# Four of twelve modulation blocks ahead of the first norm, the other eight in the merges, and each block on two column groups

## What is computed

```
mod = silu(c) @ w_mod[l] + b_mod[l]            # c: (1, 1024), w_mod[l]: (1024, 6144)
mod_c = silu(c_ctx) @ w_mod[l] + b_mod[l]
sh1, sc1, g1, sh2, sc2, g2 = split(mod, 6)
h = rmsnorm(x, norm1[l]) * (1 + sc1) + sh1     # first norm
q, k, v of three attention branches, gates = split(h @ w_in[l])
x = x + g1 * (sum over branches of sigmoid(gate_n) * (o_n @ w_branch[l][n])) @ w_out[l]
h2 = rmsnorm(x, norm2[l]) * (1 + sc2) + sh2    # second norm
x = x + g2 * moe(h2)                           # 16 experts, two for each token
```

## Time and profile before

| | |
|---|---|
| median of 3 runs | 1875.71 us (1874.19 to 1879.04) |
| the profiled execution | 1875.32 us, span 1873.7 us |
| mean granted TensorE clock | 0.964 |
| PE busy | 1696.4 us, 91% |
| DVE, ACT, POOL busy | 463.4, 339.6, 132.2 us |
| DMA | 396.74 MB, mean 212 GB/s |
| w_mod: loads | 24 of 2048 KB |
| w_mod: matmul passes (L1369) | 384, busy 170.6 us |

### The profile page before, as it was taken

How to read it: one execution, slowest core, us unless ns; L and a number is a source line. 1 busy time by engine, 2 the same in 40 slices (tenths; PEclk the granted TensorE clock), 3 DMA queues, 4 the chain that set the end, 5 groups by cost and what they waited for, 6 DMA issues and landing times. The chain is left out here.

```text
span 1873.7 us, 15998 instructions
## 1 busy us (share of the span) xinstructions
PE 1696.4 (91%) x6163; PEld 758.0 (40%) x6163; DVE 463.4 (25%) x1206; ACT 339.6 (18%) x759; POOL 132.2 (7%) x219
## 2 busy tenths in 40 slices
PE   7999998889999999999999989998799949987871
PEld 1244445554444445244444324445544424432220
DVE  0324016760011123210110145207601140011003
ACT  1011117770000012010010012017600111010001
POOL 0110000010000000210000020000200010001001
PEclk9999999999999998999999999999999969998886
DMA  9971323012213044899999997243234177999992
GB/s 337 369 250 51 90 96 141 14 28 68 78 57 134 0 147 146 332 372 357 391 387 393 395 382 232 91 113 146 55 117 155 45 279 271 323 370 385 380 393 99
DMA packets 178194, 396.74 MB, mean 212 GB/s; under 512 B 23694, under 2 KB 27822, under 8 KB 177928
## 3 DMA queue, kind: packets, MB, share of 16 engines
q1 hardware_dynamic: 160256, 327.17, 49.0%
q0 software_dynamic: 17136, 66.13, 9.5%
q10 hardware_dynamic: 724, 2.38, 0.3%
HBM read 373.27 MB, written 34.18 MB: 217 GB/s over the span
## 5 line engine op out<-in xcount | busy, mean ns | idle before, releaser
L1418 PE MATMUL bank<-ring_sb,HT_sb 128*128 128x512 f32 x672 | 297.0, 597 | 2.7 <-ACT HT_sb L701 1.5
L1483 PE MATMUL bank<-ring_sb,HT_sb 128*128 128x512 f32 x576 | 253.3, 592 | 1.4 <-ACT QR_sb L792 1.4
L1598 PE MATMUL bank<-ring_sb,QR_sb 128*64 128x512 f32 x608 | 149.7, 649 | 42.0 <-DMA ring_sb<-w_e_up 42.0
L1418 PEld LDWEIGHTS bank<-ring_sb,HT_sb 128*128 128x128 f32 x672 | 126.2, 192 | 150.2 <-issue 148.3
L1369 PE MATMUL bank<-ring_sb,cT_sb 128*2 128x512 f32 x384 | 170.6, 605 | 1.6 <-DMA ring_sb<-w_mod 1.6
L1483 PEld LDWEIGHTS bank<-ring_sb,HT_sb 128*128 128x128 f32 x576 | 109.3, 190 | 138.7 <-issue 136.8
L1487 PE MATMUL bank<-ring_sb,QR_sb 128*128 128x512 f32 x288 | 129.5, 592 | 0.0
L1598 PEld LDWEIGHTS bank<-ring_sb,QR_sb 128*64 128x64 f32 x608 | 49.8, 149 | 128.0 <-issue 127.9
L1459 PE MATMUL bank<-WK_sb,KR_sb 128*64 128x128 f32 x960 | 68.3, 280 | 36.3 <-ACT WK_sb L802 35.5
L1584 PE MATMUL bank<-ring_sb,QR_sb 128*128 128x512 f32 x208 | 94.2, 606 | 3.4 <-ACT QR_sb L838 3.4
L1614 PE MATMUL bank<-ring_sb,QR_sb 128*128 128x512 f32 x208 | 91.8, 594 | 0.0
(11 more groups left out here) (209 smaller groups left out, 1333.1 us busy)
## 6 DMA issues: line engine op xcount, KB each, us to landing
ring_sb<-w_e_gate SPq DMA_DIRECT2D x32, 2048.0 KB, 18.7
ring_sb<-w_e_up SPq DMA_DIRECT2D x32, 2048.0 KB, 21.0
ring_sb<-w_e_down SPq DMA_DIRECT2D x32, 2048.0 KB, 20.4
ring_sb<-w_mod SPq DMA_DIRECT2D x24, 2048.0 KB, 12.5
ring_sb<-w_in SPq DMA_DIRECT2D x22, 2048.0 KB, 15.7
MB_sb<-mod_d POOLq DMA_DIRECT2D x16, 512.0 KB, 8.2
ring_sb<-w_branch SPq DMA_DIRECT2D x8, 1024.0 KB, 10.1
ring_sb<-w_out SPq DMA_DIRECT2D x4, 2048.0 KB, 10.3
```

Source lines behind the costliest of these rows:

```text
L1418: ins = mm(bank[j % 4][:, :], HT[:, k, P * t:P * t + P], WR[slot][:, k], start=(k == 0), stop=(k == KD - 1))
L1483: ins = mm(bank[i % 2][:, :], HT[:, k, P * t:P * t + P], WR[wg][:, k], start=(k == 0), stop=(k == KD - 1))
L1598: ins = mm(bank[0][HALF * side:HALF * side + HALF, :], hgT[q % 2][:, k, 0:HALF], WR[slot][:, k], start=(k == 0), stop=(k == KD - 1))
```

## The change

Four things are done together.

- **c.** c and c_ctx are loaded with eight neighbouring elements in each partition, straight into the form that cT needs; the eight transposing matmuls go. A partition's rows of w_mod are then eight neighbouring ones ("(p k) n" in place of "(k p) n"). ScalarE issues all loads of X ahead of Silu. The waits of SP on c, tab and `AHEAD` go.
- **Two column groups.** A block's matmuls 0 to 3 write partitions 0 and 1 of the bank, and 4 to 7 partitions 64 and 65, in turn. VectorE adds both halves, one addition more per row. This holds for all 24 blocks.
- **The first four blocks alone.** Blocks 0 to 3 come first. Their rows are spread to 128 partitions by matmuls with a column of the identity as weights, repeated 128 times (`spread_row`, two for each row, into banks 4 to 7), and copied by ScalarE into `modb`; neither a store nor a load. The first norm of layer 0 follows, and its transposes fall between the first jobs of the projection, as in layer 1.
- **The other eight in the merges.** Block 4 + i // 2 runs after merge job i, for i = 1, 3, ... 15 (jobs count from 0), on PE, VectorE and in the order of loads. POOL loads their bias and gain after attention, stores the eight rows, and then loads gout and modb. The rows of blocks 0 to 7 of layer 1 get a place each. POOL waits for the stores of layer 1's rows ahead of `load_modb(1, 0)`.

The diff, cut:

```diff
-AHEAD = 3
-H1_ROWS = (6, 7, 8, 9)
+FIRST = 4
-MOD_BANK = (0, 1, 2, 3, 0, 1, 2, 3, 0, 1, 2, 3, 0, 4, 5, 0, 4, 5, 3, 4, 0, 1, 2, 3)
+MOD_BANK = (0, 1, 2, 3, 4, 5, 4, 5, 4, 5, 4, 5, 0, 4, 5, 0, 4, 5, 3, 4, 0, 1, 2, 3)
+def mods_after(l, i):
+    return [FIRST + i // 2] if l == 0 and i % 2 and i // 2 < NMOD - FIRST else []
...
     for l in range(L):
         order = []
-        names = [("mod", l, j) for j in range(MOD_GAP * l, NMOD)]
+        names = [("mod", l, j) for j in (range(MOD_GAP, NMOD) if l else range(FIRST))]
         names += [(u, l) for u, _ in proj_units(l)]
-        names += [(x, l) for n in range(NB) for x in (f"wb{n}", f"g{n}0", f"g{n}1")] + [("wo0", l), ("wo1", l)]
+        i = 0
+        for n in range(NB):
+            names.append((f"wb{n}", l))
+            for half in range(2):
+                names.append((f"g{n}{half}", l))
+                for t in queries(l):
+                    names += [("mod", l, j) for j in mods_after(l, i)]
+                    i += 1
+        names += [("wo0", l), ("wo1", l)]
...
-        mrow = [KR[0:2, c0:c0 + CW] for c0 in (3 * D, 3 * D + CW, D, D + CW)]
-        crow = X[0:2, 3, :]
+        mrow0 = mrow + [KR[0:2, 5 * D + CW * (j % 2):5 * D + CW * (j % 2) + CW] for j in range(FIRST, NMOD)]
+        mrow1 = [HT[0:2, j, :] for j in range(MOD_GAP)] + [mrow[j % 2] for j in range(MOD_GAP, NMOD)]
...
-                    if l == 0 and i == 1:
-                        eng.wait_ge(c_in, 32)
-                        eng.wait_ge(tab_in, 16)
-                    if l == 0 and AHEAD <= i < NMOD:
-                        eng.wait_ge(mod_mm, i - AHEAD + 1)
...
                 eng.wait_ge(pv_mm, M0 + M)
+                if l == 0:
+                    load_bmod(0, MB[0:2, 0:4 * D], FIRST)
+                    load_norm(0, 1)
+                    for j in range(FIRST, NMOD):
+                        store_mod(0, j)
                 mod_stored(NMOD * (l + 1))
                 load_gout(l, 2)
                 load_modb(l, 3)
...
+                    mod_stored(NMOD + MOD_GAP)
                     load_modb(1, 0)
...
-            eng.wait_ge(cT_mm, 1)
-            act(cT[:, :, :].rearrange("p k s -> p (k s)"), bank[7][:, 0:2 * KD], ACT.Silu).then_inc(cT_ready, 1)
...
+                if l == 0:
+                    for i in range(2 * FIRST):
+                        j, strm = divmod(i, 2)
+                        part, half = divmod(j, 2)
+                        eng.wait_ge(row_mm, i + 1)
+                        act(modb[:, strm, 1 - part, CW * half:CW * half + CW], bank[4 + i % 4][:, :], ACT.Copy)\
+                            .then_inc(row_copied, 1)
...
-                eng.wait_ge(mod_mm, i + 1)
-                n = 2 if l else 4
-                if i >= n:
-                    eng.wait_ge(mod_store[(i - n) % 4], 16 * ((i - n) // 4 + 1))
+                eng.wait_ge(mod_mm, 2 * (i + 1))
+                if j >= (MOD_GAP if l else FIRST) + 2:
+                    last_use = stored(l, j - 2)
+                    eng.wait_ge(mod_store[last_use % 4], 16 * (last_use // 4 + 1))
+                made = [bank[MOD_BANK[i]][HALF * side:HALF * side + 2, :] for side in range(2)]
+                link(tt(row, made[1], b, ALU.add))
                 if part in (1, 4):
-                    link(tt(row, made, b, ALU.add))
+                    link(tt(row, row, made[0], ALU.add))
                     stt(row, row, 1.0, nrow[l][part // 4][:, CW * half:CW * half + CW], ALU.add, ALU.mult)\
                         .then_inc(mod_row, 1)
...
+            for t in range(NT):
+                eng.wait_ge(row_copied, 2 * FIRST - 1 + t // NLAT)
+                modulated(t, hn[t % 2])
...
-                for k in range(KD):
-                    ins = mm(bank[use][0:2, :], cT[:, k, :], WR[slot][:, k], start=(k == 0), stop=(k == KD - 1))
-                ins.then_inc(mod_mm, 1)
+                for k in range(KD // 2):
+                    for side in range(2):
+                        ins = mm(bank[use][HALF * side:HALF * side + 2, :], cT[:, KD // 2 * side + k, :],
+                                 WR[slot][:, KD // 2 * side + k], start=(k == 0), stop=(k == KD // 2 - 1))
+                        if k == KD // 2 - 1:
+                            ins.then_inc(mod_mm, 1)
+            def spread_row(j):
+                eng.wait_ge(mod_row, j + 1)
+                for strm in range(2):
+                    i = 2 * j + strm
+                    if i >= 4:
+                        eng.wait_ge(row_copied, i - 3)
+                    mm(bank[4 + i % 4][:, :], ident[0:2, strm:strm + 1].broadcast_to([2, P]), mrow0[j],
+                       start=True, stop=True).then_inc(row_mm, 1)
+            for j in range(FIRST):
+                modulation(j)
+                if j == 0:
+                    eng.wait_ge(tab_in, 16)
+                else:
+                    spread_row(j - 1)
+            spread_row(FIRST - 1)
+            eng.wait_ge(row_copied, 2 * FIRST)
...
                     ins.then_inc(branch_mm, 1)
+                    for j in mods_after(l, i - before(merge_jobs, l)):
+                        modulation(NMOD * l + j)
```

More of the change, by code:

```diff
@@ L296, in build @@
         gq_in = sem("gq_in")
-        cT_mm = sem("cT_mm")
+        row_mm = sem("row_mm")
+        row_copied = sem("row_copied")
         cT_ready = sem("cT_ready")
@@ L517, in store_mod @@
                 eng.wait_ge(mod_row, i + 1)
-                dma(mod_d[l, :, CW * j:CW * j + CW], mrow[i % (2 if l else 4)]).then_inc(mod_store[i % 4], 16)
+                dma(mod_d[l, :, CW * j:CW * j + CW], mrow1[j] if l else mrow0[j]).then_inc(mod_store[stored(l, j) % 4], 16)
             def mod_stored(count):
                 for i in range(4):
-                    eng.wait_ge(mod_store[i], 4 * count)
+                    eng.wait_ge(mod_store[i], 4 * (count - FIRST))
             def load_modb(l, first):
@@ L529, in load_modb @@
                             .then_inc(modb_in, 16)
-            load_bmod(0, QR[0:2, 0:6 * D], 0)
+            load_bmod(0, QR[0:2, 0:2 * D], 0)
             load_norm(0, 0)
[L533 to L539, removed]
             dma(masks[:, :], t_in["masks"]).then_inc(const_in, 16)
@@ L716, in _ @@
                         copy_h(NT * 2 * l + t - 1, t - 1)
+                if l == 0:
[5 more added lines that the diff above has]
+                            .then_inc(row_copied, 1)
                 for t in range(NT - 1 if l else 0, NT):
                     copy_h(NT * 2 * l + t, t)
-                for i in range(4):
-                    eng.wait_ge(mod_store[i], 4 * NMOD * (l + 1))
+                if l:
+                    for i in range(4):
+                        eng.wait_ge(mod_store[i], 4 * (2 * NMOD - FIRST))
                 jobs = proj_jobs(l)
@@ L919, in mod_rows @@
                 else:
-                    tt(row, made, b, ALU.add).then_inc(mod_row, 1)
+                    tt(row, row, made[0], ALU.add).then_inc(mod_row, 1)
             n_hn = 0
@@ L943, in _ @@
             n_hsq, n_nat = 0, 0
-            for i in range(NMOD):
+            for i in range(FIRST):
                 mod_rows(i)
-                if i in H1_ROWS:
-                    t = H1_ROWS.index(i)
-                    if t == 0:
-                        eng.wait_ge(modb_in, 64)
-                    modulated(t, hn[t % 2])
+            for t in range(NT):
+                eng.wait_ge(row_copied, 2 * FIRST - 1 + t // NLAT)
+                modulated(t, hn[t % 2])
             eng.wait_ge(tab_in, 16)
@@ L1334, in arrived @@
                 return slot
-            eng.wait_ge(c_in, 32)
-            eng.wait_ge(tab_in, 16)
-            for k in range(KD):
-                ins = mm(bank[7][:, 2 * k:2 * k + 2], crow[:, P * k:P * k + P], tab[0:2, T_IDENT:T_IDENT + 2],
-                         start=True, stop=True, is_transpose=True)
-            ins.then_inc(cT_mm, 1)
             eng.wait_ge(cT_ready, 1)
@@ L1402, in _ @@
                     if j < NT:
-                        if l and j == 1:
+                        if j == 1:
                             transpose_h(1)
-                        if l and j == 2:
+                        if j == 2:
                             transpose_h(2)
```

43 lines of the change are left out of this document (22 added, 21 removed).

## The result

The changed kernel takes 1899.03 us (median, 1897.65 to 1900.23) against 1874.95 (1873.92 to 1879.04) for the kernel before on the same chip: a ratio of 1.0123, interval 1.0105 to 1.014. The profiled execution took 1898.0 us with a span of 1896.1, which is 22.4 more than before, at a mean granted clock of 0.944 and not 0.964. The forecast was 1886, with a range of 1878 to 1895 for its own case and 1868 to 1900 with the rivals B and C: slower, as forecast, but by 24 us where the working gave 10.

A forecast was written before the change was run, and what follows sets the result against it. PE was taken as the bound (busy 91%), with DMA also full in the modulation and experts. 1875.3 - 50.0 + 67.9 - 8.4 + 0.7 = 1885.5, as a median 1886; own range 1878 to 1895, with rivals 1868 to 1900.

The forecast's parts named there:

- B: Ahead of the experts PE's blocks count in full (24 us, not 8.4), or the front is at its best: 1870; chance 0.11.
- C: Front's fourth block at the lower clock and later arrival, and DMA gives nothing back in the experts: 1900; chance 0.14.
- step 2: Front: loading bounds the first four blocks; projection's first matmul at 44.8 us where it was 102.3; -50.0 us.
- Step 1: All w_mod blocks: on two column groups a block has 16 passes and takes 3.45 us, where it took 6.9.
- Step 3: Merges: slots in strict turn stall PE after jobs 7 and 15 (23.0 and 18.4 us), plus six blocks: +67.9 us.
- rival A: Merges: no stall, m7 and m11 are loaded in time; takes back 40.3 us: 1845; chance 0.04.
- Rival D: Front and merges: the new w_mod loads are slow, at 201 GB/s; 28 us more: 1913; chance 0.05.
- Step 4: Ahead of the experts: gathered rows release them; middle between PE's 9.5 and DMA's 7.1 us: -8.4, bounds 0 and -13.3.
- Step 5: End of layer 0: VectorE's row between the two tiles gets one addition: +0.7 us, up to 3.

The follow-up runs named there:

- the run with both repairs: The changed kernel with POOL's constant loads held back until the fourth row is made and w_mod loaded in the old row order: 1889.94 us (one run).

## Why the prediction was right or wrong

The mechanism was right: both holes came, at the forecast places and for the forecast reason, and they decide the sign. What failed are the sizes of four terms. At the front it is step 2's 11.3 MB at 0.39 MB/us in 29.0 us, and a term of PE that was not counted (6.4 us together); in the merges the price of the stalls, 41.4 us, which measured 45.5 (with smaller terms 5.8 us); ahead of the experts the middle between PE's and DMA's bound (−3.5 us); and in layer 1 a change put at nothing, which measured 3.3 us. The miss of 12.1 would be 15.6 without the third, which went the other way by luck.

**Step 1, price of a block: right.** Blocks follow each other at 3.53 us against the 3.45 worked out from the earlier trace rows. Weights of 2 columns cost nearly what weights of 64 do. What it is worth depends on what else bounds the stage: the run with one group is 39 us slower, of some 82 us of PE work saved (24 x 3.4), and two groups alone on the kernel before gave 14 us.

**Step 2, the front: 6.4 us too good.** The series from the fourth block on was right: 31.2 to 44.8 is 13.6 us in the forecast, and 37.96 to 51.63 is 13.7 in the trace. What failed is the sentence that 11.3 MB pass at 0.39 MB/us. The seven windows from 2 to 16 us add up to 4.2 MB, where 0.39 MB/us gives 5.5; with late constants they add up to 5.0. That rate was taken from windows in which large loads follow each other, and the constants, which were counted by their bytes ("some 0.5 MB"), cost more than that: taken out of the way, the projection starts 4.9 us earlier. The remaining 1.9 us (the fourth block at 33.08 against 31.2, the projection at 46.76 against 44.8) is a term that was missing: the spreading matmuls of rows 0 to 2 stand between the blocks on PE, 1.91 us for each row, and from the second block on PE's 5.44 us per block are the bound, in the changed kernel too (no gap from 27.08 to the end of the fourth block). In the run with both repairs the first block starts 2.2 us earlier and nothing comes of it. The loads (5.4 us for 2.10 MB at 0.39) and PE (5.44) have nearly the same pace, and the forecast counted one. One reading stays open: the working gave the slow weight loads at the start to the lower clock, but the clock column reads 1.00 there, as it does from 19 to 27 us in the changed kernel, where the first block lasts 6.38 us. That passes are slow at the start is shown; that it is the clock is not.

**Step 3, the merges: mechanism right, 5.8 us too good.** Places, order and contents of both holes are as forecast, and the run with other slots takes back 43.9 us where rival A had 40.3 for it. Rival A itself, no stall at all, falls. The terms: holes 25.1 + 20.4 = 45.5 against 41.4, so 4.1 too low; the low clock after them 3.0 + 2.5 = 5.5 against 5.8; six blocks 21.2 against 20.7; 1.6 not counted. Of the 4.1, the old row order takes back 2.9, and 0.4 is a slip of the working (2.10 MB at 201 GB/s are 10.4 us and not 10.0; the same slip makes rival D's 4.6 a 5.0). The sentence of step 2 that puts "no difference" between eight neighbouring rows and rows 128 apart is what failed: 2 KB pieces are not enough to tell a load's rate. At the head of the queue, a w_mod load made PE wait 9.8 to 10.3 us and in the old order 8.2 to 8.5.

**Rival D** was the same cause at a larger price: +28 us at 201 GB/s. The windows of the first load show 297 and 317 GB/s against 402 and 389, about a fifth to a quarter slower and not half. By the Trainium skill ("DMA: Bandwidth & Descriptors", section "Latency and other measured facts") copies between HBM tensors fall to about half rate, 103 GB/s, when their partitions lie 4 or 8 MiB apart, and still reach 207 at 512 KiB. No run here has such a distance: 192 KB is smaller and no power of two, and half rate didn't come. That the new row order is slower at the head of the queue is shown, in every run (297 to 355 GB/s from 4 to 8 us in all runs with the new order, 366 to 426 in all with the old); whether by the distance between partitions or by the pieces of one partition lying closer is not, since both changed. In a stream of loads it does not show: from 16 to 20 us the rate is 410 and 402 GB/s, and 407 and 400 in the old order.

**Step 4, ahead of the experts: 3.5 us too cautious.** The experts start 14.8 us earlier and give 2.9 back, where the forecast had 9.5 for PE's part and took the middle to the 7.1 that DMA had free. That bound did not hold: the two stages became 11.9 us shorter, and in the experts DMA moved 391 GB/s where it had moved 382. The release by the rows of hs_d and PE's idle time (12 forecast, 11.8 measured) were right. Four runs make a square of w_out to the first expert:

| | rows wait for a store | each row has its place |
|---|---|---|
| one column group | 128.5 (before) | 130.1 |
| two column groups | 124.6 | 113.7 |

Neither part alone brings much: the two groups 3.9 us, the free rows nothing (1.6 longer). With one group PE is the bound and the free rows don't help; with two groups and shared rows VectorE's wait for a store takes PE's place. The gain of 14.8 is that of both. The four kernels differ in other things ahead of this stage too, and the run with one group was measured once; what that makes in the square is not shown.

**Step 5, the end of layer 0: right**, 0.8 against 0.7. PE's idle time is the forecast 15 us, but in four pieces: 7.2 of it are waits for w_mod between the blocks, and 8.15 stand before layer 1's first transposes.

**Layer 1: 3.3 us that no step had.** The working took everything after the experts as unchanged. In the waits by cause, from layer 1's projection on, PE's row for w_e_up is the one that moved; first the changed kernel, then the kernel before:

```profile
PE bank L1635 <- DMA ring_sb<-w_e_up: 42.9, 9, 8.6
```

```profile
PE bank L1598 <- DMA ring_sb<-w_e_up: 39.4, 9, 6.7
```

The longer layer 1 comes back in the repeat (714.2), in the runs with other slots, late constants or both repairs of the loads (713.7, 714.6, 714.4), with slots and constants together (714.1) and in most part with one group (713.1), and is not there in the run with the old row order alone (710.6) nor in the kernel before with two groups (711.1). So it is not the row order alone, since with late constants on top it is back. The row for w_e_up reads 42.1 and 41.2 us in those two short ones, and only 40.1 in the long ones with other slots, where PE's busy time is 623.2 us instead of 620.6; so the waits for w_e_up don't account for it either. The cause stays open.

**Rivals B and C.** B needed the whole 24 us of PE's work ahead of the experts, or the front at its best; the stage gave 11.9 and the front 43.6. C came nearest in time (1900), but that is luck and not its mechanism: only its late arrival at the front came true, while the fourth block ran at 3.60 us, the pace of the upper clock, and the experts did give time back.

## What to carry to other kernels

When units share a ring in strict turn, a new unit takes the slot of the one that many places back; before inserting it, look for the unit that holds its slot longest and ask whether the loads behind it in the queue are wanted sooner. Here that was 44 us, and a list of 14 slot numbers took it back. A cheap stage at the start is bounded by everything that moves then, small constants too; and two repairs of one stage (shorter blocks, free rows) may each bring little and together much.

## What was not expected of the hardware

- Small loads of constants lowered the rate of the core from 411 and 401 GB/s to 306 and 229 in two windows at the start, with the DMA share near 1 either way: 4.9 us on the path for 529 KB.
- Eight neighbouring rows of 24 KB in a partition, read 2 KB at a time, gave 297 and 317 GB/s where rows 128 apart gave 402 and 389, in a load that stands at the head of the queue. In a stream of loads the rate is about 400 GB/s in both orders.
- Blocks of 16 passes on two column groups that a load released after 4.4 us or more of idle time took 4.9 to 6.5 us in these runs where they take 3.6 in a stream. After 2.2 to 3.3 us some took 3.60 and others 5.2 to 6.5: 2.34 us ahead of one of 5.30 (granted clock 0.50), 2.43 ahead of one of 3.60 (1.00). The window at 482 us in the first hole shows the granted clock at 0.50, the lower of the two levels (1.2 GHz); at the very start of the kernel the column reads 1.00 and the first block is as slow all the same.
